# Sample tokens' state updates as four 32-row products side by side, with the decays moved to GpSimd

## The reference

```python
# gated DeltaNet, per sequence b and head h
S = jnp.exp(gL_c)[..., None, None] * S + jnp.einsum('bhsk,bhsv->bhkv', k_end_c, u)
# mLSTM
C = decay[..., None, None] * C + jnp.einsum('bhsk,bhsv->bhkv', kw, v_c)
n = decay[..., None] * n + jnp.sum(kw, axis=-2)
```

## Time and profile before

| | us |
|---|---|
| median of 3 runs | 2701.01 |
| lowest, highest run | 2698.94, 2701.26 |
| span of the profiled execution | 2701.0 |
| PE busy in it | 2659.5 |
| DVE busy | 1863.6 |
| ACT busy | 1070.8 |
| POOL busy | 529.8 |

### The profile page before, as it was taken

How to read it: one execution, slowest core, us unless ns; L and a number is a source line. 1 busy time by engine, 2 the same in 40 slices (tenths; PEclk the granted TensorE clock), 3 DMA queues, 4 the chain that set the end, 5 groups by cost and what they waited for, 6 DMA issues and landing times.

```text
span 2701.0 us, 43738 instructions
## 1 busy us (share of the span) xinstructions
PE 2659.5 (98%) x18234; PEld 2619.8 (97%) x18234; DVE 1863.6 (69%) x2179; ACT 1070.8 (40%) x1559; POOL 529.8 (20%) x251
## 2 busy tenths in 40 slices
PE   9999999999999999999999999999999999999998
PEld 9999999999999799999999999999999999999998
DVE  7748386987677678476577974848666786574756
ACT  5425253243223545344345552524411254252545
POOL 2130303332010030302113302030333311102041
PEclk9999999999999799999999999999999999999999
DMA  4223223232003122223232232232222223232231
GB/s 133 84 72 85 79 75 90 57 79 55 17 9 87 56 86 79 79 79 94 63 90 69 82 91 71 80 92 75 85 79 77 63 79 94 63 97 66 81 103 49
DMA packets 401148, 205.57 MB, mean 76 GB/s; under 512 B 15554, under 2 KB 398939, under 8 KB 400952
## 3 DMA queue, kind: packets, MB, share of 16 engines
q1 hardware_dynamic: 400746, 202.70, 26.4%
q10 hardware_dynamic: 206, 0.08, 0.0%
HBM read 195.14 MB, written 7.60 MB: 75 GB/s over the span
## 4 chain that ended last, share of the span: by engine, by line
PE 81%; DVE 15%; ACT 2%; issue 1%; DMA 0%; POOL 0%; DVEq 0%; SPq 0%; ACTq 0%
PE ps L913 12%; PE ps L917 12%; PE ps L928 12%; PE ps L914 12%; PE ps L930 12%; PE ps L929 12%; PE ps L1062 3%; PE ps L1088 2%; DVE ut L2207 1%; DVE x L2941 1%; DVE ct L2996 1%; DVE r L2392 1%; DVE ct L2993 1%; DVE sumsq L2306 1%; PE ps L1056 1%
## 5 line engine op out<-in xcount | busy, mean ns | idle before, releaser
L861 POOL TENSOR_TENSOR wlo<-raw,whi 128x1024 fp32r<-128x1024 f32 (+2 forms) x214 | 518.3, 2425 | 2131.9 <-ACT whi L1637 2131.7
L913 PE MATMUL ps<-xh,whi 128*128 128x320 f32 x1552 | 472.3, 312 | 8.0 <-POOL wlo L861 5.8
L914 PE MATMUL ps<-xl,whi 128*128 128x320 f32 x1552 | 467.0, 309 | 0.0
L913 PE MATMUL ps<-hh,whi 128*128 128x320 f32 x1440 | 436.3, 311 | 4.1 <-POOL wlo L861 1.9
L914 PE MATMUL ps<-hl,whi 128*128 128x320 f32 x1440 | 433.6, 309 | 0.0
L928 PE MATMUL ps<-tau_hi,whi 128*128 128x320 f32 x1280 | 396.4, 310 | 2.9 <-DVE wlo L2223 2.0
L929 PE MATMUL ps<-tau_lo,whi 128*128 128x320 f32 x1280 | 395.5, 309 | 0.0
L930 PE MATMUL ps<-tau_hi,wlo 128*128 128x320 f32 x1280 | 395.5, 309 | 0.0
L1637 ACT CAST whi<-raw 128x1024 fp32r<-128x1024 f32 (+2 forms) x216 | 208.5, 967 | 390.8 <-PE ps L917 352.0
L917 PE MATMUL ps<-xh,wlo 128*128 128x320 f32 x1552 | 353.4, 309 | 0.0
L917 PE MATMUL ps<-hh,wlo 128*128 128x320 f32 x1440 | 328.1, 309 | 0.0
(11 more groups left out here) (435 smaller groups left out, 4827.5 us busy)
## 6 DMA issues: line engine op xcount, KB each, us to landing
raw<-in_ffn_w_gu SPq DMA_DIRECT2D x320, 256.0 KB, 3.8
raw<-in_ffn_w_d SPq DMA_DIRECT2D x64, 512.0 KB, 4.0
raw<-in_w_in_even SPq DMA_DIRECT2D x32, 512.0 KB, 4.1
raw<-in_ffn_w_d SPq DMA_DIRECT2D x32, 384.0 KB, 3.6
raw<-in_w_in_odd SPq DMA_DIRECT2D x24, 512.0 KB, 3.7
raw<-in_ffn_w_gu SPq DMA_DIRECT2D x16, 512.0 KB, 4.2
raw<-in_w_ple_gate SPq DMA_DIRECT2D x16, 512.0 KB, 3.8
raw<-in_w_out_even SPq DMA_DIRECT2D x8, 512.0 KB, 4.4
```

What stands on the lines that cost most here:

```text
L861: pool.tensor_tensor(ring(wlo, n), raw[:, slot, 0:kt, :], ring(whi, n).bitcast(fp32), ALU.subtract).then_inc(lo_ready, 1)
L913: pe.matmul(ps[j % 4][:, c, 0:HT], wh[:, k], hi[:, k, cs], start=(k == 0), stop=False)
L914: pe.matmul(ps[j % 4][:, c, 0:HT], wh[:, k], lo[:, k, cs], start=False, stop=False)
```

## The change

Each of the array's four groups of 32 rows holds the tokens of two sequences. The change makes one product per group: 32 rows of keys against 256 columns, the columns being the values of its first sequence and those of its second. So the spread of a head needs two blocks instead of eight, one for the even sequences and one for the odd. `parity`, two columns made from `bmask` with two additions on POOL at the start, takes the place of `bmask` in it. Each `spread_*` is now done once for all heads, in two activations. The four products of a head go to four different banks (2 to 5, which are `ps[1]` and `ps[2]`), so a call of `state_c` or `state_s` does two heads and fills both tiles. The additions read two banks each.

C and S products now share the same banks, so they take turns: state_c(0), state_s(0), state_c(2), state_s(2), each waiting for the additions of the pair before. The decays of the DeltaNet states go to POOL (`decays`). nsum goes to bank 0.

```diff
+        fold = sb("fold", [P, DECB // 2])
+        parity = sb("parity", [P, 2])
...
+        spread_u = W9[:, 6:8, :].rearrange("p a b -> p (a b)")[:, 0:2 * HA * P].rearrange("p (s h v) -> p s h v", s=2, h=HA)
+        spread_v = spread_c[:].rearrange("p (s h) v -> p s h v", s=2)
+        def quad(r):
+            return slice(32 * r, 32 * r + 32)
+        def pair_of(r, i):
+            return bank(2 + r)[:, i * 2 * P:(i + 1) * 2 * P]
...
+            def decays():
+                pool.wait_ge(core["ks"], NTILE)
+                for h in range(HA):
+                    ends = W(2)[:, h].rearrange("p (b t) -> p b t", t=DECT)[:, :, DECT - 1:DECT].to_broadcast([P, DECB, P])
+                    pool.tensor_tensor(sg[:, h], sg[:, h], ends, ALU.mult).then_inc(s_decayed, 1)
...
                 sample_part("den")
-                state_c(1)
-                sample_part("nsum")
                 o_sums(0)
+                sample_part("nsum")
                 state_s(0)
-                state_c(2)
                 o_spread(0)
-                state_s(1)
                 o_spread(1)
-                state_c(3)
+                state_c(2)
                 o_spread(2)
-                state_s(2)
                 o_spread(3)
+                pe.wait_ge(ms_dve, MS_DVE.index("n") + 1)
                 o_sums(HA)
-                state_s(3)
+                state_s(2)
...
-                    pe.wait_ge(c_added, h)
-                for c in range(2):
-                    last = pe.matmul(ps[1][:, c, :], VS(6)[:, h], spread_v(h)[:, c * 4:(c + 1) * 4, :], start=True, stop=True)
+                    pe.wait_ge(s_added, h)
+                for h_ in (h, h + 1):
+                    for r_ in range(4):
+                        last = pe.matmul(pair_of(r_, h_ - h), VS(6)[quad(r_), h_], spread_v[quad(r_), :, h_], start=True, stop=True)
                 last.then_inc(c_product, 1)
...
+                pe.wait_ge(c_added, h + 2)
+                for h_ in (h, h + 1):
+                    for r_ in range(4):
+                        last = pe.matmul(pair_of(r_, h_ - h), W(3)[quad(r_), h_], spread_u[quad(r_), :, h_], start=True, stop=True)
                 last.then_inc(core["sup"], 1)
...
                 own(dve.tensor_tensor(bv, heads(7), VS(0), ALU.mult).then_inc(o_new, 1), o_new)
-                add_c(1)
+                add_s(0)
+                add_s(1)
...
                 inverse(0)
-                add_s(0)
                 normalise(0)
+                normalise(1)
                 add_c(2)
-                normalise(1)
-                add_s(1)
+                add_c(3)
                 normalise(2)
-                add_c(3)
                 normalise(3)
                 add_s(2)
                 low(0)
                 low(1)
+                add_s(3)
                 low(2)
                 inverse(1)
-                add_s(3)
                 normalise(4)
```

More of the change, by code:

```diff
@@ L309, in stream_step @@
         s_added = sem("s_added")
+        s_decayed = sem("s_decayed")
         p_kept = sem("p_kept")
@@ L842, in _ @@
             select(bmask[:], [[DECT, DECB]], DECT - 1, -1, ALU.is_ge)
+            step(pool.tensor_tensor(fold[:], bmask[:, 0:DECB // 2], bmask[:, DECB // 2:], ALU.add))
+            step(pool.tensor_tensor(parity[:], fold[:, 0:2], fold[:, 2:4], ALU.add))
             def levels():
@@ L870, in _ @@
                     levels()
+                if n == core_stage["z0"] + 9:
+                    decays()
                 if blocks[n][0][0] is None:
@@ L1289, in sample_tile @@
                 sample_part("den")
-                state_c(1)
+                o_sums(0)
                 sample_part("nsum")
-                o_sums(0)
                 state_s(0)
+                o_spread(0)
+                o_spread(1)
                 state_c(2)
-                o_spread(0)
-                state_s(1)
-                o_spread(1)
-                state_c(3)
                 o_spread(2)
+                o_spread(3)
+                pe.wait_ge(ms_dve, MS_DVE.index("n") + 1)
+                o_sums(HA)
                 state_s(2)
-                o_spread(3)
-                o_sums(HA)
-                state_s(3)
             def first_blocks(s):
@@ L1348, in state_s @@
                 if h == 0:
[L1350 to L1359, removed]
+                    pe.wait_ge(core["uexp"], 1)
+                pe.wait_ge(c_added, h + 2)
+                for h_ in (h, h + 1):
+                    for r_ in range(4):
+                        last = pe.matmul(pair_of(r_, h_ - h), W(3)[quad(r_), h_], spread_u[quad(r_), :, h_], start=True, stop=True)
                 last.then_inc(core["sup"], 1)
@@ L1416, in sample_part @@
                 else:
-                    pe.wait_ge(z_out, 4 * (NTILE - 1))
                     for h in range(HB):
-                        last = pe.matmul(bank(5)[:, h * DECB:(h + 1) * DECB], VS(6)[:, h], bmask[:], start=True, stop=True)
+                        last = pe.matmul(bank(0)[:, h * DECB:(h + 1) * DECB], VS(6)[:, h], bmask[:], start=True, stop=True)
                 last.then_inc(ms_pe, 1)
@@ L2040, in _, with spread_state, spread_correction @@
                     li = (LVL - 1) * t
[L2042 to L2048, removed]
+                    def spread_state():
+                        for q in range(2):
+                            last = act.activation(spread_v[:, q], VS(5), ACT.Copy, scale=parity[:, q:q + 1])
                         last.then_inc(v_spread, 1)
[L2051 to L2055, removed]
+                    def spread_correction():
+                        for q in range(2):
+                            last = act.activation(spread_u[:, q], W(1), ACT.Copy, scale=parity[:, q:q + 1])
                         last.then_inc(core["uexp"], 1)
@@ L2659, in sample_tile @@
                 add_c(0)
-                own(dve.tensor_tensor(spread_u(0), W(1)[:, 0].unsqueeze(1).to_broadcast([P, DECB, P]),
-                                      bmask[:].unsqueeze(2).to_broadcast([P, DECB, P]), ALU.mult).then_inc(u_first, 1), u_first)
+                add_c(1)
                 decay_c(2)
@@ L2674, in sample_tile @@
                 mul(W(0)[:, :, 0:DECB], n_, ends)
-                ms(dve.tensor_tensor(n_, W(0)[:, :, 0:DECB], bank(5)[:, 0:HB * DECB].rearrange("p (h b) -> p h b", h=HB), ALU.add))
+                ms(dve.tensor_tensor(n_, W(0)[:, :, 0:DECB], bank(0)[:, 0:HB * DECB].rearrange("p (h b) -> p h b", h=HB), ALU.add))
                 dve.sem_inc(ms_dve, 1)
```

41 lines of the change are left out of this document (14 added, 27 removed).

## The result

The changed kernel takes 2720.64 us (median of 4 runs, 2719.72 to 2722.60) against 2701.14 us before (2698.94 to 2702.36). The ratio is 1.0073, with a 95% interval of 1.0061 to 1.0086. It is slower by 19.5 us. The forecast, 2712.6 us, had the sign and lies 8 us too low, and the measured time is above the range given, which ended at 2719.0.

The account below looks back on a forecast made before the run. The prediction took TensorE (PE), busy 98% of the span, as the bound. Waits +6.2, first clock term +3.2 and second +2.2 sum to +11.6 on a 2701.0 us span: 2712.6 us, range 2706.5 to 2719.0.

Parts of the forecast that it names:

- The waits: PE idle 4.3 us before o_spread(0) and 6.5 us before o_spread(4), waiting for DVE's reciprocals; +6.2 us at unchanged clock.
- Rival A: The forecast itself: waits moved onto DVE before inverse(0) and inverse(1), clock falling in both pauses; +11.6 us, chance 0.50.
- The price p of a pair: PE time for two heads' state products on 32-row tiles: taken as 1.9 us, bounds 0.85 and 3.4.
- Rival C: 32-row tiles of the state products do not overlap; +11.9 us, with both clock terms +17; chance 0.14.
- rival D: Tiles go side by side and the clock holds; p = 0.85 gives +4.1 us, DVE's additions keep the rest; chance 0.10.
- Up to the denominators: Nothing moves much: state_c(0) does two heads in 3.3 us against 3.16; denominators end at 910.3.
- Rival E: Faster: denser PE work lifts the clock in stretches that were at half; -4.4 to about -6.7 us, chance 0.04.
- From there to o_spread(4): Walk from denominators ending at 910.3 to o_spread(4) at 947.25, before the first clock term's +3.2 us.
- The first clock term: Half clock after the first pause: o_spread(0) and o_spread(1) +1.1 us each, state_c(2) +1.0; +3.2 us.
- The second clock term (b): Half clock after the pause before o_spread(4), at least 6.8 us, 4.4 us of it on first_blocks; +2.2 us.
- POOL: Four decays moved from DVE take 10 to 13 us from 882.7 us, done by about 896; DVE's saved 5.0 us worth 0.
- ACT: the worth of 0: Seven spreads replaced by two on ACT, which waits for PE anyway: worth 0, up to 14.8 us of ACT time if uncovered.

Follow-up runs that it names:

- reordered run: Changed kernel with its lists reordered so neither reciprocal stands behind additions needing a late product; 2702.20 us, ratio 1.0008.
- the kernel before with the pause: Kernel before with 128-row o_spread and a PE pause made by putting add_s(3) and three low ahead of inverse(1); 2702.11 us, ratio 1.0004.
- the kernel with a filled pause: Changed kernel with seven unused products of 512 columns put into PE's second pause, ahead of o_spread(4); 2714.00 us, ratio 1.0049.

## Why the prediction was right, and where it was wrong

**The waits: right.** Both stood where the forecast put them, released by the reciprocals, with 5.64 us against 4.3 and 6.67 against 6.5. Rival A had the mechanism, and its size was too small. The reordered run shows what the order costs: with the reciprocals ahead, 18.4 us come back.

**The price p of a pair: mis-sized.** Forecast 1.9 us, measured 1.12. Sixteen passes follow each other much faster than my argument from issue order and the 0.106 us per weight load allowed. From 16 to 48 passes the group grows from 1.08 to 2.80 us, so 0.86 us per pair, which is the bound of 0.85 for four tiles side by side. Rival C, tiles that do not overlap, is out. For one group the figure of the Trainium skill ("TensorE: Matmul & The Clock Gate", Part 3), 3.07 times for four tiles of 512 columns, agrees: a pair of heads took 2 x 1.72 = 3.44 us before, and 3.44 / 1.12 = 3.07. The size of p made little difference, as rival D said. The two later pairs that are not covered are 0.8 us shorter each.

**Up to the denominators: forecast +0.1, measured -4.3.** At the same clock the product is only 0.6 us of it (1.08 us for a pair, where one full head takes 1.72). The other 3.7 us are the clock. In the changed kernel it was at full from 894.8 to 901.6 us, and before only from 901.6 to 905.0, so state_c(0) itself ran at half there. This is mostly chance of the execution. Of the four profiles whose program is that of the kernel before up to this point, the denominators end between 904.0 and 910.0 us, and in the eight that have the changed program up to it between 902.1 and 908.6. The two profiles compared here happen to lie far apart. Rival E named such a rise, but as a faster kernel it did not come.

**From there to o_spread(4): forecast 40.2 us, measured 42.9.** The first clock term was right that the clock falls in the pause. It was mis-sized: I let it be back for o_spread(3) and o_sums(HA). It stayed at half for 23.9 us, so o_spread(3) took 2.9 instead of 1.53 us and o_sums(HA) 6.3 instead of 4.5. DVE's slow product added 1.0 us, and the shorter pairs took 1.6 back.

**The second clock term (b): this step failed.** It says "a half-clock stretch of at least 6.8 us, the shortest row, begins inside the idle time. Some 4.4 us of it falls on work of first_blocks, which takes twice as long: +2.2". Measured: 24.4 us of work at half clock, and +10.8 us up to DVE's first use of the output projection. The 8.6 us between them are about the whole of the 8 by which the forecast was off. The other errors, -4.4 up to the denominators, +2.7 behind them and +1.4 at the end, nearly cancel. I took the shortest of the stretches before as typical and did not ask what the work behind the pause would do to the clock. In the first 20 us of first_blocks o_spread takes more than half of it, and the runs show that with 24 rows the clock came back there after 24.4 us of work, or came back and fell again. With 128 rows it was back after 5.8 and 3.4 us of work (in the changed kernel, and in the kernel before with the pause) and stayed. A time above 2719 had a chance of some 0.05, and for another reason, rival C.

**POOL: right. ACT: the worth of 0 missed 1.0 us of pause before o_spread(0).** POOL's decays took 7.97 us, from 882.64 us, well under the 10 to 13 forecast, and moving them back changed nothing. ACT waited 5.76 us for the denominators, as said. But a relieved ACT ran its cast 6.5 us earlier, counted from the denominators, and POOL's subtraction behind it slowed a product of DVE in front of inverse(0). The forecast named the slowing and did not ask where the subtraction would now fall.

**What stays open.** The kernel before holds full clock through the same four 24-row o_spread, and the kernel with a filled pause lost it there without a gap. What differs between the two at that point was not found. That 128 rows in place of 24 shorten the time at half clock is shown by one edit in three kernels (the changed one, the reordered one and the kernel before with the pause). In the kernel before, the clock was at full either way. Whether it is the rows or the 0.39 us at each group, and how much either weighs, was not measured.

## What to carry to other kernels

When a product gets shorter, ask what its result is queued behind. Here additions in front of two reciprocals left PE idle for 5.64 and 6.67 us, and with the waits gone the saved product time was worth about a microsecond. The pauses of 3.4 to 6.7 us in these profiles cost their own length and then a half-clock stretch behind them. How long that lasted depended on the work that followed: size it by what stands there, never by the shortest stretch in another place. When an engine is relieved, ask also what it will now do earlier, and what that collides with. Small products with few rows among full ones are worth a try padded to 128 rows with zero weights. It gave 4.7 us in the kernel before, 10.9 us in the changed one and 7.4 us in the reordered one.

## What the runs showed of the hardware

- Four 32-row tiles run side by side in fp32, both passes included: 16 passes of 256 columns in 1.08 us, 48 in 2.80, where one 512-column pass on 128 rows takes 0.43. With three such groups of 48 in a stretch of 27.2 us the granted clock stood at 1.00.
- A group of twelve 24-row passes between 128-row products costs 0.39 us more than the same group on 128 rows.
- The granted clock stayed at half for 27.3 us (24.4 of them busy) in the changed kernel and for 30.7 us (28.0 busy) in the reordered one, with 24-row products among PE's work. With 128-row ones in the same places it was 10.2 us (5.8 busy) and 3.4 us (all busy).
- POOL multiplies a 128x1024 tile by a broadcast operand in 2.0 us. While it subtracts, a 32-column product of two SBUF operands on DVE takes 1.20 instead of 0.21 us.
